# An expert stage with weights as the stationary operand in fp32, in place of weights split in two and streamed past the tokens

## The reference, cut to what matters

```python
logits = h @ w_router + b_router              # 512 tokens, 32 experts, all float32
top_v, top_i = lax.top_k(logits, 4); gate = softmax(top_v)
# every token goes to 4 experts; the tokens of one expert are worked on in blocks
gu  = xb @ w_gu[e] + b_gu[e]                  # (rows,1024) x (1024,2048)
g   = minimum(gu[:, :1024], 7.0)
lin = clip(gu[:, 1024:], -7.0, 7.0)
act = g * sigmoid(1.702 * g) * (lin + 1.0)
y   = act @ w_down[e] + b_down[e]             # (rows,1024) x (1024,1024)
x  += segment_sum(y * gate)                   # back to the tokens
```

## Time and profile before

| what | value |
|---|---|
| median of three runs | 1909.05 us |
| span of the profiled execution, first to last instruction | 1905.7 us |
| between the two | 3.35 us (no time of the profiled execution alone is listed beside its span) |
| TensorE busy | 1698.8 us, 89% |
| VectorE, ScalarE, GpSimd busy | 76%, 57%, 40% |
| moved by DMA | 480 MB, mean 252 GB/s |
| first expert matmul to last | 500.4 to 1881.9 us |

### The profile page before, as it was taken

The page is one execution under the profiler, slowest core; times in us unless marked ns, Lnnn a source line. Parts: engine busy times, 40 slices in busy tenths (PEclk is TensorE's granted clock), DMA queues, the critical chain, the costliest instruction groups (busy, mean ns, idle before and its releaser), DMA issues.

```text
span 1905.7 us, 23153 instructions
## 1 busy us (share of the span) xinstructions
PE 1698.8 (89%) x7877; PEld 1241.3 (65%) x7877; DVE 1457.7 (76%) x1432; ACT 1095.5 (57%) x1073; POOL 753.9 (40%) x293
## 2 busy tenths in 40 slices
PE   6999999998798989898888989898988989898984
PEld 5877788886566666666566666666656666666662
DVE  5665624355788888888888888888888888888886
ACT  4366722233366666665666565666656666666654
POOL 7200000002244545555444554455554445455452
PEclk9999999999799999999989999999998999999997
DMA  8220013257489989888888998888988989988893
GB/s 268 85 66 2 1 55 116 65 204 257 149 311 316 323 292 323 305 304 318 309 288 309 321 319 308 309 304 307 318 312 281 316 316 319 312 318 293 303 324 132
DMA packets 202067, 480.13 MB, mean 252 GB/s; under 512 B 10977, under 2 KB 11505, under 8 KB 201905
## 3 DMA queue, kind: packets, MB, share of 16 engines
q1 hardware_dynamic: 193824, 452.36, 66.1%
q0 software_dynamic: 7888, 27.23, 6.3%
q10 hardware_dynamic: 320, 0.08, 0.0%
HBM read 460.86 MB, written 19.66 MB: 252 GB/s over the span
## 4 chain that ended last, share of the span: by engine, by line
PE 58%; issue 14%; DVE 14%; ACT 12%; DMA 1%; ACTq 0%; DVEq 0%; SPq 0%; POOLq 0%; POOL 0%
PE ps L1321 16%; PE ps L1322 16%; PE ps L1323 15%; DVE act_sb L1278 9%; ACT w_high L772 7%; PE ps L1346 5%; PE ps L1440 2%; PE ps L1570 1%; PE ps L1414 1%; DVE act_sb L1276 1%; DVE sg_sb L1300 1%; ACT sg_sb L839 1%; ACT L772 1%; ACT L839 1%; ACT y_sb L846 1%
## 5 line engine op out<-in xcount | busy, mean ns | idle before, releaser
L1096 DVE TENSOR_TENSOR w_low<-w_raw,w_high 128x2048 fp32r<-128x2048 f32 x289 | 790.8, 2737 | 121.7 <-ACT w_high L772 118.2
L903 POOL TENSOR_TENSOR w_low<-w_raw,w_high 128x2048 fp32r<-128x2048 f32 x99 | 515.4, 5206 | 806.5 <-ACT w_high L772 806.0
L772 ACT ACTIVATE w_high<-w_raw 128x2048 fp32r<-128x2048 f32 x388 | 729.9, 1908 | 64.4 <-PE ps L1323 64.1
L1321 PE MATMUL ps<-w_high,xt_hi 128*96 128x512 f32 x1024 | 455.7, 445 | 0.3 <-DVE xt_lo L1257 0.3
L1322 PE MATMUL ps<-w_low,xt_hi 128*96 128x512 f32 x1024 | 423.4, 414 | 0.0
L1323 PE MATMUL ps<-w_high,xt_lo 128*96 128x512 f32 x1024 | 422.9, 413 | 0.0
L830 ACT ACTIVATE at_hi<-ps 128x384 fp32r<-128x384 f32 x64 | 31.5, 492 | 359.6 <-PE ps L1346 359.6
L1322 PEld LDWEIGHTS ps<-w_low,xt_hi 128*96 128x96 f32 x1024 | 177.7, 174 | 79.6 <-issue 0.6
L1321 PEld LDWEIGHTS ps<-w_high,xt_hi 128*96 128x96 f32 x1024 | 179.1, 175 | 76.8 <-issue 1.2
L1323 PEld LDWEIGHTS ps<-w_high,xt_lo 128*96 128x96 f32 x1024 | 176.1, 172 | 79.4 <-issue 1.1
L1321 PE MATMUL ps<-w_high,at_hi 128*96 128x512 f32 x512 | 212.5, 415 | 0.0
(11 more groups left out here) (228 smaller groups left out, 2050.7 us busy)
## 6 DMA issues: line engine op xcount, KB each, us to landing
w_raw<-in_w_gate_up SPq DMA_DIRECT2D x260, 1024.0 KB, 7.1
w_raw<-in_w_down SPq DMA_DIRECT2D x128, 1024.0 KB, 5.6
w_raw<-in_w_in SPq DMA_DIRECT2D x8, 2048.0 KB, 9.2
w_raw<-in_w_out SPq DMA_DIRECT2D x2, 2048.0 KB, 8.3
x_sb<-in_x SPq DMA_DIRECT2D x4, 512.0 KB, 6.5
w_raw<-in_w_in SPq DMA_DIRECT2D x2, 1024.0 KB, 16.9
w_raw<-in_w_mem_kv SPq DMA_DIRECT2D x1, 2048.0 KB, 13.9
x<-in_x SPq DMA_DIRECT2D x4, 512.0 KB, 5.0
```

The source lines that it names most:

```text
L772: nc.scalar.activation(half_of(wh, m, SPLIT_SLOTS), half_of(raw, m, RAW_SLOTS), ACT.Copy).then_inc(wh_done, 1)
L903: nc.gpsimd.tensor_tensor(half_of(wl, m, SPLIT_SLOTS), half_of(raw, m, RAW_SLOTS), half_of(wh, m, SPLIT_SLOTS).bitcast(F32), ALU.subtract) ...
L1096: nc.vector.tensor_tensor(half_of(wl, m, SPLIT_SLOTS), half_of(raw, m, RAW_SLOTS), half_of(wh, m, SPLIT_SLOTS).bitcast(F32), ALU.subtract) ...
L1321: nc.tensor.matmul(bank, hi, w_hi, start=start, stop=False)
```

## The change

The weights are no longer split. Each raw float32 tile of 128 x 128 weights is itself the stationary operand of a float32 matmul, and the transposed tokens (128 x 96, float32) move past it; so results come out transposed (features on partitions, tokens along the free axis), the activation feeds the down product without a transpose, and only the final y is turned back (8 transposes). Biases are added per partition by VectorE, from a table `bias_job` that TensorE makes ahead of the loop (24 float32 matmuls of 55 columns). Which tokens fill which job is worked out for all jobs ahead of the loop (`slot_rows`, `slot_gates`: 16 float32 matmuls of 110 columns, from VectorE's `job_hots`, `slot_hot`, `job_vals`), and `slots`, `bias`, `moe_high`, `moe_low`, `pool_low` and `turn_act` are gone. Weights have 16 gate/up slots of 1 MiB (two jobs) and 4 down slots of 1 MiB (one job). TensorE's order is gate/up of jobs 0 and 1, then in the loop down(j), gate/up(j+2).

Weight slots in SBUF:

```diff
-        PARTS, HALF = 12, UNIT // 2
-        RAW_SLOTS, SPLIT_SLOTS = 8, 6
+        gu_w = [sb(f"gu_w{i}", [P, 2 * D], F32, at * KIB)
+                for i, at in enumerate((64, 72, 80, 88, 96, 104, 0, 8, 32, 40, 48, 56, 16, 24, 112, 120))]
+        dn_w = [sb(f"dn_w{i}", [P, 2, D], F32, (128 + 8 * i) * KIB) for i in range(4)]
```

SyncE:

```diff
+            sp.wait_ge(slots_ready, 1)
+            for k in range(4):
+                load_gu(e1, 1, k)
+            sp.wait_ge(bias_ps, 1)
+            for k in range(4, KD):
+                load_gu(e1, 1, k)
...
+                    for k in range(KD):
+                        sp.wait_ge(gu_ps, value(i, KD, b * KD + k + 1))
+                        load_gu(e_gu, b, k)
+                    for q in range(DN_PARTS):
+                        sp.wait_ge(dn_ps, value(i, DN_PARTS, b * DN_PARTS + q + 1))
+                        load_dn(e_dn, q)
```

ScalarE, in the loop:

```diff
-                        moe_high(i, b * PARTS + p + LEAD)
+                    sigmoids(i * 2 + (b + 1))
+                    keep_gate(i * 2 + b, b)
+                    take_xt(i * 2 + (b + 2), b)
+                    take_y(i * 2 + b, b)
```

VectorE, ahead of the loop: tables of all jobs:

```diff
+            for t in range(TB):
+                c = slice(t * TOP_K, (t + 1) * TOP_K)
+                step.inc(nc.vector.tensor_tensor(job_hots[:, c, :], numbers(NJ), spread(dest_jobf[:, c], NJ), ALU.is_equal))
+                step.inc(nc.vector.tensor_tensor(slot_hot[:, c, :], numbers(SLOTS), spread(dest_slot[:, c], SLOTS), ALU.is_equal))
+                dve.wait_ge(dve_chain, step.n)
+                step.inc(nc.vector.tensor_tensor(job_vals[:, c, 0, :], job_hots[:, c, :], spread(dest_vals[:, c, 0], NJ), ALU.mult))
+                nc.vector.tensor_tensor(job_vals[:, c, 1, :], job_hots[:, c, :], spread(dest_vals[:, c, 1], NJ), ALU.mult).then_inc(vals_ready, 1)
```

VectorE, in the loop:

```diff
+            def activate(j, b):
+
+                dve.wait_ge(gu_ps, j * KD + KD)
+                for h in range(2):
+                    n = j * 2 + h
+                    g, sg, lin = g_sb[:, h, :, :], sg_sb[:, h, :, :], act_t[b][:, h * QUAD:(h + 1) * QUAD, :]
+                    nc.vector.tensor_tensor(g, bank(2 * h), biases(h, j), ALU.add).then_inc(g_added, 1)
+                    nc.vector.tensor_tensor(lin, bank(2 * h + 1), biases(2 + h, j), ALU.add).then_inc(l_added, 1)
...
+                    activate(i * 2 + (b + 1), 1 - b)
+                    take_xt(i * 2 + (b + 2), b)
+                    take_yt(i * 2 + b)
```

TensorE:

```diff
+                for k in range(KD):
+                    pe.wait_ge(gu_in[b * KD + k], m)
+                    for n in range(4):
+                        for c in range(QUAD):
+                            f = (n // 2) * QUAD + c
+                            last = nc.tensor.matmul(ps[:, n, c * SLOTS:(c + 1) * SLOTS],
+                                                    gu_w[b * KD + k][:, (n % 2) * D + f * P:(n % 2) * D + (f + 1) * P],
+                                                    xt[b][:, k, :], start=k == 0 and c == 0, stop=k == KD - 1, skip_group_check=True)
+                    last.then_inc(gu_ps, 1)
+                    between(k)
...
-                    for p in range(PARTS):
...
+                    down(j, b, value(i, 16, (b + 1) * 16), next_tokens)
+                    pe.wait_ge(l_added, j * 2 + 4)
+                    gate_up(j + 2, b, i * 16 + 32, rows_of_y)
```

More of the change, by code:

```diff
@@ L233, in encoder_kernel @@
[L233 to L242, removed]
@@ L289, in encoder_kernel @@
         first_in = sem("first_in")
-        part_in = [sem(f"part_in{i}") for i in range(8)]
+        gu_in = [sem(f"gu_in{i}") for i in range(16)]
+        dn_in = [sem(f"dn_in{i}") for i in range(4)]
         x2_in = sem("x2_in")
@@ L1531, in _ @@
                 turn_logits(t)
-            def slots(n):
-                pe.wait_ge(slot_hot_ready, n + 1)
-                for t in range(TB):
-                    last = nc.tensor.matmul(ps[0:SLOTS, 7, 0:4], slot_hot[:, t, :], slot_rhs[:, t, :], start=t == 0, stop=t == TB - 1)
-                last.then_inc(slot_ps, 1)
             pe.wait_ge(chosen_ready, 1)
@@ L1569, in bias @@
-            def bias(bank, s, table, n):
-                nc.tensor.matmul(bank, expert_b[:, s, :], table[:, n:n + COLS], start=True, stop=False)
-            pe.wait_ge(slot_ready, 1)
-            pe.wait_ge(table_ready, 1)
-            pe.wait_ge(wl_pool, LEAD - 1)
+            for c in range(CHOICES):
+                pe.wait_ge(vals_ready, c // TOP_K + 1)
+                last = nc.tensor.matmul(ps[0:SLOTS, 3, 0:2 * NJ], slot_hot[:, c, :], job_vals[:, c, :, :].rearrange("p v j -> p (v j)"),
+                                        start=c == 0, stop=c == CHOICES - 1)
@@ new lines, in _, with turn_tokens, gate_up @@
+            last.then_inc(slots_ps, 1)
+            pe.wait_ge(hot_ready, 1)
+            nc.tensor.matmul(ps[0:1, 2, 0:NJ], cols[0:N_EXP, 6:7], job_hot[:], start=True, stop=True).then_inc(hot_ps, 1)
+            def turn_tokens(j, b):
+                for h in range(2):
+                    for k in range(QUAD):
+                        last = turn(6 + h, k * SLOTS, xg[b][:, (QUAD * h + k) * P:(QUAD * h + k + 1) * P])
+                    last.then_inc(x_ps, 1)
+            def gate_up(j, b, m, between):
+                pe.wait_ge(xt_a, j + 1)
+                pe.wait_ge(xt_d, j + 1)
+                for k in range(KD):
[8 more added lines that the diff above has]
+                    between(k)
@@ new lines, in down @@
+            def down(j, b, m, between):
+                for q in range(DN_PARTS):
+                    pe.wait_ge(dn_in[q], m)
+                    if q % 2 == 0:
+                        pe.wait_ge(act_ready, j * 2 + q // 2 + 1)
+                    for k in range(2):
+                        for n in range(2):
+                            for c in range(QUAD):
+                                d = n * QUAD + c
+                                last = nc.tensor.matmul(ps[:, 4 + n, c * SLOTS:(c + 1) * SLOTS], dn_w[q][:, k, d * P:(d + 1) * P],
+                                                        act_t[b][:, 2 * q + k, :], start=q == k == c == 0, stop=q == DN_PARTS - 1 and k == 1,
+                                                        skip_group_check=True)
+                    last.then_inc(dn_ps, 1)
+                    between(q)
@@ new lines, in turn_y @@
+            def turn_y(j):
+                for h in range(2):
+                    pe.wait_ge(yt_ready, j * 2 + h + 1)
+                    for c in range(QUAD):
+                        last = turn(6 + h, c * P, y_t2[:, h * QUAD + c, :])
+                    last.then_inc(y_tp, 1)
+            pe.wait_ge(slots_ready, 1)
+            pe.wait_ge(table_ready, 1)
+            pe.wait_ge(bias_in, 32)
+            for n in range(3):
+                for c in range(KD):
+                    last = nc.tensor.matmul(ps[:, 3 + n, c * NJ:(c + 1) * NJ], bias_f[:, (n * KD + c) * P:(n * KD + c + 1) * P], job_hot[:],
+                                            start=True, stop=True, skip_group_check=True)
```

583 lines of the change are left out of this document (238 added, 345 removed).

## The result

The changed kernel took 1948.95 us in the median of 4 runs (1948.28 to 1950.47), the kernel before 1909.53 (1908.17 to 1914.02): a ratio of 1.0207, 95% interval 1.0192 to 1.0222. It is slower, by about 2%; the forecast was 1964 us with a range from 1938 to 2008. The profiled execution took 1950.47 us, its span is 1948.6.

What follows compares the result with a forecast made beforehand. TensorE was taken as the bound, DMA nearly full. 45.8 for 32 jobs, less 0.9, + 5.6 + 3 + 1.9 = +55.4 on a span of 1905.7; with 3.35 for the median, about 1964 us, range 1938 to 2008.

Steps and rivals of the forecast that it cites:

- Price of a pass and of a job: Expert loop on TensorE: 0.112 us a pass, set by the weight load; 44.6 us a job, 1.4 more than before.
- upper neighbour: Attention's probabilities times values, 128 columns loaded and 128 moved: 0.112 us a pass, taken as the price from above.
- first rival: Expert loop: load hidden or short, passes of 0.082 us, DMA the bound at 38.5 us a job, about 1770 us; chance 0.10.
- No wait and full clock in the loop: Expert loop: after the change nothing waits, so TensorE runs at full clock and no clock term is added.
- First to last expert matmul: Expert loop: 45.8 for 32 jobs, less 0.9 for the last y transposes, plus 3 for emptying banks before gate/up(1).
- The start, +5.6: Ahead of the loop: gate/up(0) starts at about 506 us instead of 500.4; bounds +0 to +8.
- The contention of the earlier trace: Ahead of the loop: two small VectorE operations lay on GpSimd's `w_low`, TensorE waited 4.80 us; removing it gains 4.8.
- The tables: Ahead of the loop: some 16 VectorE operations for the tables of all jobs, about +5 us.
- Behind the last matmul: Tail after the last expert matmul: a bias add and 4 to 8 transposes come between, +1.9 us.
- DMA at nothing: Expert loop: a job's 13.4 MB need 38.5 us at full share, below 44.6, so DMA adds no time.
- Jump back: Loop end: a longer TensorE body might be fetched anew at each of 15 jumps, +30 to +90 us; chance 0.08.
- the wait of the earlier trace: Expert loop before: activation transposes waited 135.7 us for VectorE's `act_sb`, 4.2 us a job, which the change removes.

Runs made afterwards that it cites:

- load96: The changed kernel with each expert matmul loading 96 of its 128 weight columns, all transfers kept: 1620.38 us.
- n128: The changed kernel with each expert matmul moving 128 token columns instead of 96: 1950.58 us.
- n48: The changed kernel with each expert matmul moving 48 token columns instead of 96: 3234.88 us.
- start_arith: The changed kernel with the six bias loads at the start and GpSimd's copies and subtractions on them put back: 1956.16 us.
- b_dve: The kernel before with GpSimd's share of the weight splitting given to VectorE, same output: 1788.98 us, ratio 0.9374.
- half_mm: The changed kernel with every second expert matmul left out and all transfers kept: 1571.36 us.

## Why the prediction was right, and where not

- **Price of a pass and of a job**: 0.112 us and 44.6 us, as forecast from the earlier trace rows. The reason was right too: the load sets it, and `load96`, `n128` and `n48` agree. What the prediction left open is how near the stream is: 0.083 us at 96 columns and 0.111 at 128, so that its upper neighbour is bound by both. The Trainium skill (FP8 and Floating Point Precision, TensorE Precision Notes) counts four passes for true float32, and the float32 rows of 512 and 128 moved columns above agree: two records a matmul, each at twice the fp32r price. By this count alone, as an estimate, the new matmul would take 0.160 us; it took 0.224, since the load is the longer of the two. Two slips of the prediction changed nothing: its own terms give 42.5 us for the lower bound of a job and not 42.7 (or 42.9, as under the first rival), and the VectorE operations of 384 elements, put near 0.38 us, took 0.55.
- **No wait and full clock in the loop**: right. The one bubble between gate/up(0) and gate/up(1), forecast at 3 us, was 2.65 us (`act_t`), with some 4 us at or near half clock behind it.
- **First to last expert matmul**: 45.8 - 0.9 + 3 = +47.9 forecast, +46.2 measured.
- **The start, +5.6, was the step that failed**: -4.7 was measured, some 10 of the 15 us by which the forecast of 1964 was too high. Three terms were off. The largest was missing: the diff also removes six loads and GpSimd's arithmetic from the first 50 us, and I costed the edits of the expert stage only; that is -6.6 at the last norm, and `start_arith`, which has them back, starts its experts at 501.9 and not 495.8. The contention of the earlier trace rows, -4.8 by TensorE's wait, was 13.1 - 6.6 = 6.5. And from the rows of job 0 to gate/up(0) I had 15 us where it took 13.2, as the bias matmuls took 9.0 instead of 10.3. The tables, forecast +5, cost 13.1 - 8.2 = 4.9.
- **Behind the last matmul**: +1.9 forecast, +1.3 measured. The forecast then put the median 3.35 us above the profiled span; it stands 0.35 above it, another 3 us of the miss. The time lay inside the range because the start, wrong in sign, is small beside the 46 us of the loop.
- **DMA at nothing**: right for the changed kernel (share 0.82), with a wrong floor, 38.5 us a job instead of 34. It made the price of the first rival wrong: with passes of 0.085 us `load96` took 1620 us, not 1770.
- **Jump back**: no gap anywhere in the loop; the rival fell.
- **What I read past**: the prediction took the wait of the earlier trace rows for the price of splitting, and the change as the trade of this wait against passes. `b_dve` shows that this wait was the price of giving GpSimd a share of the splitting: without it the wait was gone, one of half the length was left elsewhere, and the kernel was 120 us faster with its old matmuls.

## What to carry to other kernels

A float32 matmul with a small moving tile is priced by its weight load, so count passes by the columns loaded, and let the moving side fill up to them; from there on (128 loaded, 128 moved here) the stream has the same price. Before you trade one engine's work for another's, look at the minimum and the maximum of the operations that are waited for, not at the mean: an operation of 0.7 us that takes 5.1 beside another engine is a wait, and removing the neighbour can be worth more than the trade (here 120 us gained against 39 lost). And cost what a diff removes at the far end of the program too, its loads in the first microseconds above all.

## What the runs showed of the hardware

- The granted clock was 0.50 through the expert stage of `n48`, 2.7 ms, with TensorE busy 100% from 600 us on and 48 columns moved per pass; with 96 columns and the same loads it was 1.00. A stream without gaps was thus not at full clock for that alone.
- Float32 records of 512 moved columns stood 0.439 us apart, of 128 columns with 32 loaded 0.111; with 128 loaded and 96 or 128 moved it was 0.112 (the whole kernel 1948.95 and 1950.58 us).
- VectorE's operations were longer beside GpSimd's arithmetic: 0.687 us became 5.1 and 0.15 became 3.46 beside `w_low`, 2.29 became 3.86 (`start_arith`) and 4.48 (before) beside the bias splitting of the first 30 us.
- With gate/up weights in 8 KB rows DMA moved 391 to 395 GB/s at a full share (`load96`, `half_mm`); with 2 KB rows 339 at 0.98 (`b_dve`).
